# Maxima and exponentials of a dilated attention unit ahead of the eviction of a normed piece

## The reference, cut to what matters

```python
xn = rms_norm(x, norm1_g)
proj = xn @ w_in
qa = partial_rotary(rms_norm(a_q.reshape(shp), a_qn_g), cos, sin)   # 3 groups, 6 heads of 64
ka = partial_rotary(rms_norm(a_k.reshape(shp), a_kn_g), cos, sin)
va = a_v.reshape(shp)
for g, (window, dil) in enumerate(((128, 1), (512, 4), (2048, 16))):
    o_g, l_g = dilated_window_attention(qa[:, :, g], ka[:, :, g], va[:, :, g], dil, window // (2 * dil))

# inside dilated_window_attention, per block of queries
s = where(mask, q @ k.T / 8, -1e30)
mx = max(s); p = exp(s - mx); den = sum(p)
o = (p / den) @ v
```

## Time and profile before

| what | value |
|---|---|
| median of 3 runs | 3232.37 us (3230.68 to 3233.95) |
| the profiled execution | 3235.13 us, of it span 3233.4 us |
| TensorE busy | 3142.3 us, 97% of the span |
| VectorE busy | 1539.6 us, 48% |
| ScalarE busy | 1185.4 us, 37% |
| chain that ended last | PE 79%, DVE 9%, ACT 6%, issue 4%, DMA 2% |

### The profile page before, as it was taken

One profiled execution on the slowest core, in us unless ns is written; L12 is line 12 of the kernel. 1 busy time (PEld: TensorE's weight loads), 2 busy tenths in 40 slices (PEclk: granted clock), 3 DMA queues, 4 the chain that ended last, 5 costly groups with the idle time before them and its releaser, 6 DMA issues.

```text
span 3233.4 us, 45389 instructions
## 1 busy us (share of the span) xinstructions
PE 3142.3 (97%) x17652; PEld 2888.0 (89%) x17652; DVE 1539.6 (48%) x3149; ACT 1185.4 (37%) x2656; POOL 509.7 (16%) x879
## 2 busy tenths in 40 slices
PE   7999998999999999999999999989999999999999
PEld 7999888888888999999999998888888889999998
DVE  4445236654465343433465452466545643433434
ACT  4334434465632211211243444344755322211211
POOL 1111421222252000000012124212222510000000
PEclk9999999999999999999999999999999999999999
DMA  5334444443385221212234344434333832212212
GB/s 192 116 118 130 130 138 130 130 131 116 98 214 168 66 60 58 78 45 72 66 128 131 94 138 141 140 115 143 119 114 125 213 131 66 78 47 70 77 40 72
DMA packets 273371, 358.51 MB, mean 111 GB/s; under 512 B 27440, under 2 KB 209904, under 8 KB 273192
## 3 DMA queue, kind: packets, MB, share of 16 engines
q1 hardware_dynamic: 213640, 179.41, 18.8%
q0 software_dynamic: 59552, 176.68, 17.6%
HBM read 264.42 MB, written 91.59 MB: 110 GB/s over the span
## 4 chain that ended last, share of the span: by engine, by line
PE 79%; DVE 9%; ACT 6%; issue 4%; DMA 2%; POOL 1%; SPq 0%; ACTq 0%; DVEq 0%; POOLq 0%
PE ps L1989 21%; PE ps L1913 16%; PE ps L1915 16%; PE ps L1914 16%; PE ps L2060 2%; PE ps L2108 1%; PE ps L2134 1%; DVE wl L1499 1%; PE ps L2045 1%; PE ps L2034 1%; ACT arena L1296 1%; PE ps L2022 1%; PE ps L2156 1%; DVE stage L1543 1%; DVE stage L1540 1%
## 5 line engine op out<-in xcount | busy, mean ns | idle before, releaser
L1913 PE MATMUL ps<-wh,xh 128*128 128x384 f32 (+1 forms) x1440 | 529.6, 368 | 3.9 <-DVE stage L1578 1.9
L1915 PE MATMUL ps<-wh,xl 128*128 128x384 f32 (+1 forms) x1440 | 515.2, 358 | 0.0
L1914 PE MATMUL ps<-wl,xh 128*128 128x384 f32 (+1 forms) x1440 | 514.3, 357 | 0.0
L1913 PE MATMUL ps<-xh,wh 128*128 128x384 f32 (+1 forms) x1312 | 459.0, 350 | 35.0 <-ACT stage L1205 21.3
L1915 PE MATMUL ps<-xh,wl 128*128 128x384 f32 (+1 forms) x1312 | 443.3, 338 | 0.0
L1914 PE MATMUL ps<-xl,wh 128*128 128x384 f32 (+1 forms) x1312 | 443.2, 338 | 0.0
L1499 DVE TENSOR_TENSOR wl<-wraw,wh 128x1024 fp32r<-128x1024 f32 (+2 forms) x210 | 232.4, 1111 | 429.7 <-ACT wh L1194 429.7
L1989 PE MATMUL ps<-xl,wh 128*128 128x384 f32 x1280 | 325.0, 334 | 0.0
L1989 PE MATMUL ps<-xh,wl 128*128 128x384 f32 x1280 | 324.9, 334 | 0.0
L1989 PE MATMUL ps<-xh,wh 128*128 128x384 f32 x1280 | 324.7, 334 | 0.0
L1863 DVE SCALAR_TENSOR_TENSOR arena<-arena,ps 128x768 f32<-128x768 f32 x44 | 42.0, 954 | 546.1 <-ACT arena L1448 546.1
(11 more groups left out here) (230 smaller groups left out, 5183.2 us busy)
## 6 DMA issues: line engine op xcount, KB each, us to landing
wraw<-in_w_in SPq DMA_DIRECT2D x96, 512.0 KB, 3.9
wraw<-in_w_ffn_in SPq DMA_DIRECT2D x88, 512.0 KB, 4.4
wraw<-in_w_in SPq DMA_DIRECT2D x72, 384.0 KB, 3.3
wraw<-in_w_ffn_out SPq DMA_DIRECT2D x44, 512.0 KB, 3.9
qkv_a<-stage POOLq DMA_DIRECT2D x108, 192.0 KB, 2.2
gate_t<-stage POOLq DMA_DIRECT2D x96, 192.0 KB, 2.2
stage<-gate_t POOLq DMA_DIRECT2D x78, 192.0 KB, 4.3
mix_t<-stage POOLq DMA_DIRECT2D x52, 192.0 KB, 4.1
```

The source lines that it names most:

```text
L1913: pe.matmul(out, ah, bh, start=first, stop=False)
L1914: pe.matmul(out, ah, bl, start=False, stop=False)
L1915: return pe.matmul(out, al, bh, start=False, stop=last)
```

## The change

A second list, `EVICT_STEPS`, is made from `STEPS`. When an `a_out` or `a_score` comes and the last dense step put into the list is a normed piece, the side step is inserted ahead of that piece. VectorE and ScalarE now walk through the new list; TensorE, GpSimd and SyncE keep the old one. No instruction is added or removed, and no semaphore changes.

```diff
+def evict_order(steps):
+
+    order = []
+    for i, s in enumerate(steps):
+        if s in INDEX:
+            last = len(order)
+        if s[0] in ("a_out", "a_score") and order and order[last] in HEADS:
+            order.insert(last, s)
+            last += 1
+        else:
+            order.append(s)
+    return order
+
+
+EVICT_STEPS = evict_order(STEPS)
...
-                    for step in (NEXT_STEPS if layer else FIRST_STEPS) + STEPS:
+                    for step in (NEXT_STEPS if layer else FIRST_STEPS) + EVICT_STEPS:
...
-                    for step in (NEXT_STEPS if layer else FIRST_STEPS) + STEPS:
+                    for step in (NEXT_STEPS if layer else FIRST_STEPS) + EVICT_STEPS:
```

## The result

| kernel | median us | runs | ratio to before, 95% interval |
|---|---|---|---|
| before | 3231.52 | 8 (3228.15 to 3235.21) | |
| changed | 3242.44 | 8 (3238.07 to 3248.28) | 1.0031 (1.0022 to 1.0040) |

What follows compares the result with a forecast made beforehand. TensorE, busy 97% of the span, was taken as the bound: 8.77 us of new waits against 6.46 removed gave +2.31 per layer, +4.6 in all. That meant 3239.7 profiled, 3237.0 on the median, range 3230.5 to 3242.

Steps and rivals of the forecast that it cites:

- the likeliest class: Whole kernel: result within about 0.2% (6.5 us) of before, on the slow side; chance 0.69.
- All seven waits at `a_turn` go: TensorE's transposes, seven per layer: exponentials end by S + 2.8, wanted at S + 4.30; the waits delay starts by 5.84 us.
- New waits at `a_out`: TensorE per layer: transposed-part copy behind two evictions instead of one makes 8.77 us of new waits at seven units.
- The signs in the profile: TensorE's waits: `a_turn` row vanishes, `a_out` row has six or seven per layer, about 7.5 us, longest about 2.2 and 1.7.
- Units 6 and 14 get none: `a_out` there: a plain piece VectorE does not evict follows, chain some 3 us shorter, so no wait.
- What goes: TensorE: seven `a_turn` waits, longer waited transposes and a hidden `a_out` wait at unit 12; 6.46 us per layer.
- Bounds: Unseen effects: restart of a waited `a_out` 0 to 0.8 us, taken as 0; eviction overlap or ScalarE lateness, ends -4 and +7.
- rival 2: `a_fold` 9: loads arrive late, TensorE waits 2.1 us more per layer; +8.8 in all, 3241.2; chance 0.10.
- Rival 1: TensorE: all waits go and none comes, -12.9 us, 3219.5; chance 0.05.
- Rival 3: VectorE: second eviction overlaps ScalarE's answers, chain 0.3 to 0.6 shorter per slot; -3.8 to +0.4, about 3231; chance 0.15.

Runs made afterwards that it cites:

- e4: Changed kernel with VectorE's weight splits of pieces (8,0), (8,3) and (8,4) put behind its copy of the transposed part: 3230.28 us, 0.9996 of before.
- e6: Kernel before with only the scores of units 6 and 14 moved, with the output copies before them: 3232.67 us, 1.0000 of before.
- e3: Changed kernel with the move kept only for six-head scores, units 12 and up: 3241.16 us, 1.0026 of before.
- e1: Changed kernel with VectorE's and ScalarE's copies of the transposed part (`a_turn`) also moved ahead of the normed piece: 3218.89 us, 0.9956 of before.
- e5: Kernel moving only scores below unit 12, plus three chained VectorE copies ahead of its transposed-part copy at units 5 and 11: 3252.08 us, 1.0058 of before.
- e7: Kernel before with only the copies of the transposed part (`a_turn`) moved ahead of the normed piece: 3233.45 us, 0.9998 of before.
- e2: Changed kernel with the move kept only for three-head scores, units below 12, with their output copies: 3236.18 us, 1.0013 of before.

## Why the prediction came out as it did

Against the kernel before beside it the change costs 10.9 us, where I forecast 4.6 with a range of -1.9 to +9.6; as a time, 3242.44 stands 0.4 above the upper end of 3242.0. The direction was right. The size was off by 6.3 us, and the likeliest class was wrong: the interval of the ratio (1.0022 to 1.0040) lies above 1.002, so the change is slower by more than a measurement leaves open, for which I had given 0.25.

Point by point:

- All seven waits at `a_turn` go: right.
- New waits at `a_out`, by unit. Measured is by how much the start of `a_out` moved against the kernel before in layer 0; of unit 12's, 0.2 were there before:

| unit | forecast | measured in layer 0 |
|---|---|---|
| 3 | 0.29 | 0.31 |
| 4 | 0.94 | 0.95 |
| 5 | 1.16 | 1.16 |
| 10 | 0.94 | 0.96 |
| 11 | 1.16 | 1.17 |
| 12 | 1.90 | 1.91 |
| 13 | 2.38 | 2.40 |
| sum | 8.77 | 8.86 |

- The signs in the profile: six waits per layer, 15.1 us by the bracket in two layers against about 7.5 each forecast, the longest 2.2 and 1.7. Only the releaser is not named as forecast ("issue" instead of VectorE's copy); the rows of unit 13 above and e4, which moves only work of VectorE, show that it is VectorE's copy.
- Units 6 and 14 get none: right, and e6 shows it alone.
- What goes: forecast 6.46 per layer, measured 6.30. The net is +3.0 per layer (TensorE goes from 1.03 us ahead of before at unit 3 to 1.97 behind it after unit 14) where I had +2.31. Most of the 0.7 is a term that I put at nothing: under "Bounds" I took 0 for the restart, but a waited `a_out` takes 0.07 us more to the next step (313.19 to 314.64, 1.45 against 1.38). I took the 0 from unit 12 in the earlier trace rows, where `a_out` waited already; at the other six it is 0.44 in all. The waits that go are 0.16 short of the forecast, and the new ones 0.09 above it. Together +6.0 instead of +4.6 in both layers.
- The failed step is what the bounds left out: that an idle TensorE may come back at its lower clock. I let each new wait cost its own length, and the prediction has no term for the clock. Its rows could not show one: the kernel before waits 2.3 us once in each layer, in layer 0 in the earlier trace rows, without a slow stretch behind it (granted clock 1.00 from 170 to 345 us and from 1775 to 1950). In the changed kernel each layer has two waits of 1.7 and 2.2 us, some 24 us apart, and behind them TensorE ran at half clock in 2 of 4 places in the first profile and 4 of 4 in the second. e3 isolates them: 1.2 us of waits, 9.3 us of time. The 4.9 us between +6.0 and +10.9 are what the granted clock of the timed runs gives for them, about 5 (24.3 against 19.2 to 19.5). The +6.0 of the waits alone would have lain inside the range. That the measured time stands so near its upper end is luck: I had put that end at rival 2, late loads, which did not come.
- Rival 1 (all waits go and none comes, 3219.5) was wrong for this change, and e1 reached its time by the missing half: 3218.9. Its price had been 12.9, and e1 measures 13.0. The rule of the Trainium skill behind this rival (Perfetto Trace Analysis, Optimization Strategy), to find what the gaps of the busiest engine wait for and make that start sooner, held in e1, where the copies start sooner as well as the exponentials (0.9956), and not in the change, which starts the exponentials sooner and the copies later (1.0031).
- Rival 2 (late loads at `a_fold` 9): no wait at `a_fold` in the trace. Rival 3 (evictions that overlap): the second eviction at unit 13 took the full 308.49 to 311.53, 3.04 us.

What stays open: what decides whether a given wait is followed by a slow stretch. Counted over the ten profiles, waits at `a_out` of units 12 and 13 (1.7 to 2.2 us) were followed by one in 10 of 12 cases, the lengthened ones of 2.2 us in e5 in 2 of 4 (unit 11, not unit 5), waits of 2.3 us at `a_turn` of unit 13 in 4 of 10 (both layers of e5 and of e7), waits at `a_out` of 1.0 us and less (by the bracket) in 2 cases of some fifty, and the shorter waits at `a_turn` in none. So the length of the wait seems to matter; what else does, no experiment here tells.

## What to carry to other kernels

When a step is moved ahead of another one in an engine's queue, follow the moved unit to its next stop on the same engine: what was one eviction between maxima and copy became two, and the wait came back one step later and larger. Move the whole chain of the unit (maxima and copy), or nothing. And where the busiest engine is TensorE, price an added wait of about 2 us at its length plus, as seen here, nothing to some 3 us for the half clock behind it; many waits of up to 1 us (e2, 4.3 us slower than before) were cheaper than two of 2 us per layer with the same sum (e3, 9.3 us slower), though by the waits alone e3 should have been the cheaper one (+1.2 against about +5), as it removes more of them at `a_turn`. And one profile can miss such stretches: the granted clock of all timed runs shows them better.

## What the runs showed of the hardware

- Behind most waits of TensorE of 1.7 to 2.2 us at `a_out` the granted clock of a window of 5 us fell to between 0.5 and 0.8, with matmul starts 0.32 us apart instead of 0.17. The lower clock stood for some 3 to 7 us, and a stretch cost 1.6 to 3.1 us. It can stand while the DMAs are idle (e7 from 1912 to 1915 us: granted clock 0.50, DMA share 0.00).
- The same program with the same waits had two slow stretches among the dilated units in one profiled execution and five in the other. The timed runs of the changed kernel spread over 10.2 us, those of before beside them over 7.1. The mean granted clock of its timed runs lay between 0.991 and 0.994.
